# Around the second block's first norm, three units on each side run one half of the positions and then the other

## What is computed

```python
# end of the first block
f = (jax.nn.gelu(g, approximate=True) * a) @ w_down[l]      # (256, 2816) @ (2816, 1024)
x = x + rms_norm(f, norm_ffn_post[l])
# start of the second block
u = rmsnorm(x, norm_mix_g[l])
proj = u @ w_in[l]
(gq, gk, gv, gz, ga, gb, fq, fk, fv, ff, gate_a, gate_b) = jnp.split(proj, split_idx, axis=-1)
# both norms
y = xf * lax.rsqrt(jnp.mean(xf * xf, axis=-1, keepdims=True) + EPS)
return (y * g.astype(jnp.float32)).astype(x.dtype)
```

## Time and profile before

| | |
|---|---|
| median of 3 runs | 936.53 us (933.61 to 938.68) |
| the profiled execution, its own time | 933.1 us |
| its span, first to last instruction | 931.4 us |
| PE busy | 909.3 us, 98% of the span |
| DVE busy | 569.3 us, 61% |
| ACT busy | 498.1 us, 53% |
| POOL busy | 155.3 us, 17% |
| mean granted clock of TensorE | 0.998 |

### The profile page before, as it was taken

The page is one execution under the profiler, slowest core; times in us unless marked ns, Lnnn a source line. Parts: engine busy times, 40 slices in busy tenths (PEclk is TensorE's granted clock), DMA queues, the critical chain, the costliest instruction groups (busy, mean ns, idle before and its releaser), DMA issues.

```text
span 931.4 us, 15769 instructions
## 1 busy us (share of the span) xinstructions
PE 909.3 (98%) x6525; PEld 839.0 (90%) x6525; DVE 569.3 (61%) x817; ACT 498.1 (53%) x747; POOL 155.3 (17%) x169
## 2 busy tenths in 40 slices
PE   7999999999999999899999999999999999999998
PEld 7998999889999988787789997999999899998886
DVE  5556554778888753676446688765466665555442
ACT  5576864556665543557555673432545565564341
POOL 6011101511111100236634210000100001120000
PEclk9999999999999999999999999999999999999999
DMA  8743265565565556324534444632346547556560
GB/s 287 243 155 113 92 226 178 185 208 180 191 208 191 167 187 214 110 92 154 175 124 137 136 138 135 182 107 92 92 140 221 181 145 218 183 195 211 180 203 24
DMA packets 132123, 153.71 MB, mean 165 GB/s; under 512 B 9281, under 2 KB 105940, under 8 KB 132052
## 3 DMA queue, kind: packets, MB, share of 16 engines
q1 hardware_dynamic: 125684, 151.25, 50.3%
q10 hardware_dynamic: 6368, 1.45, 0.7%
HBM read 150.46 MB, written 2.23 MB: 164 GB/s over the span
## 4 chain that ended last, share of the span: by engine, by line
PE 85%; DVE 7%; ACT 3%; DMA 2%; issue 2%; POOL 1%; ACTq 0%; SPq 0%; POOLq 0%
PE ps L1830 75%; PE ps L1793 5%; PE ps L2046 2%; PE ps L1790 2%; DVE wl L798 2%; DVE gv L824 1%; ACT wh L1338 1%; DMA raw<-in_w_in 1%; DVE mt L1210 1%; DVE gv__83 L1040 0%; DMA U<-blocks 0%; PE ps L2022 0%; DVE xres L824 0%; DMA inverses<-Y 0%; ACT fg L1476 0%
## 5 line engine op out<-in xcount | busy, mean ns | idle before, releaser
L798 DVE TENSOR_TENSOR wl<-raw,wh 128x1024 fp32r<-128x1024 f32 (+1 forms) x272 | 323.8, 1206 | 202.6 <-ACT wh L1338 202.4
L1830 PE MATMUL ps<-xh,wh 128*128 128x256 f32 x1280 | 361.7, 283 | 1.4 <-ACT xh L1377 1.4
L1830 PE MATMUL ps<-xh,wl 128*128 128x256 f32 x1280 | 354.7, 277 | 1.2 <-DVE wl L798 1.2
L1830 PE MATMUL ps<-xl,wh 128*128 128x256 f32 x1280 | 351.5, 277 | 0.0
L1338 ACT ACTIVATE wh<-raw 128x1024 fp32r<-128x1024 f32 (+1 forms) x292 | 286.8, 1024 | 117.6 <-PE ps L1830 110.2
L1830 PEld LDWEIGHTS ps<-xh,wh 128*128 128x128 f32 x1280 | 241.3, 189 | 5.1 <-issue 2.4
L1830 PEld LDWEIGHTS ps<-xh,wl 128*128 128x128 f32 x1280 | 240.3, 188 | 1.6 <-DVE wl L798 1.6
L1830 PEld LDWEIGHTS ps<-xl,wh 128*128 128x128 f32 x1280 | 239.3, 188 | 0.3
L620 POOL TENSOR_TENSOR wl<-raw,wh 128x1024 fp32r<-128x1024 f32 (+1 forms) x20 | 53.0, 2649 | 76.6 <-ACT wh L1338 75.4
L1830 PE MATMUL ps<-wh,f2L 128*128 128x512 f32 x128 | 49.8, 389 | 0.0
L1830 PE MATMUL ps<-wh,f2H 128*128 128x512 f32 x128 | 49.8, 389 | 0.0
(11 more groups left out here) (316 smaller groups left out, 1371.3 us busy)
## 6 DMA issues: line engine op xcount, KB each, us to landing
raw<-in_w_in SPq DMA_DIRECT2D x56, 1024.0 KB, 5.0
raw<-in_w_up SPq DMA_DIRECT2D x38, 1024.0 KB, 5.2
raw<-in_w_down SPq DMA_DIRECT2D x26, 1024.0 KB, 5.0
raw<-in_w_out SPq DMA_DIRECT2D x8, 1024.0 KB, 5.0
raw<-in_w_proj_fox SPq DMA_DIRECT2D x4, 1024.0 KB, 5.3
raw<-in_w_proj_gdn SPq DMA_DIRECT2D x4, 1024.0 KB, 5.0
raw<-in_w_conv_branch SPq DMA_DIRECT2D x4, 512.0 KB, 3.4
raw<-in_w_att_branch SPq DMA_DIRECT2D x4, 512.0 KB, 3.3
```

The source lines that it names most:

```text
L798: e.tensor_tensor(L, R, H.bitcast(F32), ALU.subtract).then_inc(lo.sem)
L1830: k = e.matmul(o, l, r, start=opens, stop=done and n == ends[c], skip_group_check=True)
```

## The change

**PE's order.** Units 63, 64 and 65 (AHEAD2) now run for positions a = 0 first, all three, and then all three for a = 1. So do units 66, 67 and 68 (BEHIND2). A new function `part` issues the 12 matmuls of one unit and one half: all chunks high by high, the first two chunks with the low weights, all chunks with the low activations, the last two chunks with the low weights. The transposes of the norm (`x2_turn(a, h)`, four channel chunks of one half of positions) stand between these matmuls: (0, 0) before the last three of unit 65, (0, 1) in the middle of unit 66's first half, (1, 0) behind unit 68's first half, (1, 1) in the middle of unit 66's second half. The `warm` products of this norm are gone.

**The norm by halves.** The gain is now multiplied into XS by DVE (`x2_scaled`, with the row GN, loaded by one more DMA of 512 KB behind the first block's middle norm), and XH and XL are made in four pieces of 4 chunks by 128 positions (`x2_high`, `x2_low`), each from one PSUM bank.

**The other engines.** ACT, DVE and POOL have the order of this stretch written out. The second `low` halves of units 66 and 68 move to POOL; that of unit 67 stays with DVE, at another place. `small` begins behind unit 68 in place of unit 66. In the down projection the short unit (2 chunks) is now the first of a group, so units 59 and 65 have 4 chunks.

```diff
-POOL_HALF = frozenset([*range(26, 33), *range(74, 87)])
-LATE_LO = frozenset([33, 67])
+POOL_HALF = frozenset([*range(26, 33), 66, 68, *range(74, 87)])
+LATE_LO = frozenset([33])
...
-                unit_of(w_down[0], 4 * P * n, 4 if n < 5 else 2, 512 * i, "A",
-                        [pfg("fg", 4 + 2 * i + a) for a in range(2)] if n == 5 else None, k0=4 * n, first=n == 0)
+                k0 = max(4 * n - 2, 0)
+                unit_of(w_down[0], k0 * P, 4 if n else 2, 512 * i, "A",
+                        [pfg("fg", 4 + 2 * i + a) for a in range(2)] if n == 5 else None, k0=k0, first=n == 0)
...
+            e.dma_start(GN[:], norm_mix_g_2[0].partition_broadcast(P)).then_inc(ld_gn, 16)
...
@@ gpsimd
-            after_post(1)
+            for a in range(2):
+                rstd(prs, a, ss[:, 2 + a:3 + a], pred("sum", 2 + a))
+                e.wait_ge(*px("x", 2 + a))
+                rstd(nrs, a, ss[:, a:a + 1], nsq("sq", 4 + a))
+                low(U_FQ + 2 * a)
...
@@ vector
+            def x2_scaled(a):
+                e.wait_ge(*nrs("pow", 4 + a))
+                e.wait_ge(ld_gn, 16)
+                for k in (0, 512):
+                    e.scalar_tensor_tensor(XS[:, a, k:k + 512], XRES[:, a, k:k + 512], rs[:, 2 + a:3 + a], GN[:, k:k + 512],
+                                           ALU.mult, ALU.mult).then_inc(nsc.sem)
+
+            def x2_low(a, h):
+                e.wait_ge(*x2h("hi", 2 * a + h))
+                e.tensor_tensor(x2_part(XL, a, h), x2_ps(a, h), x2_part(XH, a, h).bitcast(F32), ALU.subtract).then_inc(x2l.sem)
...
+            post(1, U_FQ - 1, 1, 0)
+            low(U_FQ, 0)
+            x2_scaled(0)
+            low(U_FQ + 1, 0)
+            x2_low(0, 0)
+            post(1, U_FQ - 1, 1, 1)
+            x2_low(0, 1)
+            low(U_FQ + 1, 1)
+            low(U_FQ + 2, 0)
+            x2_scaled(1)
+            x2_low(1, 0)
+            x2_low(1, 1)
...
@@ scalar
+            post(1, U_FQ - 1, 1, 0)
+            e.wait_ge(*px("x", 2))
+            squares(0)
+            high(U_FQ, 0)
+            high(U_FQ, 1)
+            high(U_FQ + 1, 0)
+            x2_high(0, 0)
+            post(1, U_FQ - 1, 1, 1)
+            high(U_FQ + 1, 1)
+            x2_high(0, 1)
+            high(U_FQ + 2, 0)
+            e.wait_ge(*px("x", 3))
+            squares(1)
+            high(U_FQ + 2, 1)
+            keep_fqk(0)
+            x2_high(1, 0)
+            x2_high(1, 1)
...
@@ tensor
-            warm(WARM[0])
-            norm(2)
+            for a in range(2):
+                for u in AHEAD2:
+                    part(u, a, fH, fL, lambda a, q: fhi("hi", q // 2), lambda a, q: flo("lo", q // 2),
+                         at=3 if (u, a) == (U_FQ - 1, 1) else None, begins=lambda: x2_turn(0, 0))
+            part(U_FQ, 0, XH, XL, x2_hi, x2_lo, at=2, begins=lambda: x2_turn(0, 1))
+            part(U_FQ + 1, 0, XH, XL, x2_hi, x2_lo)
+            side.add(fox_norm(0))
+            part(U_FQ + 2, 0, XH, XL, x2_hi, x2_lo)
+            x2_turn(1, 0)
+            part(U_FQ, 1, XH, XL, x2_hi, x2_lo, at=2, begins=lambda: x2_turn(1, 1))
+            part(U_FQ + 1, 1, XH, XL, x2_hi, x2_lo)
+            side.add(fox_norm(1))
+            part(U_FQ + 2, 1, XH, XL, x2_hi, x2_lo)
             side.add(small())
```

214 lines of the change are left out of this document (155 added, 59 removed).

## The result

The changed kernel is slower: median 946.22 us (939.0 to 951.1, nine runs) against 937.2 (933.61 to 939.03, nine runs) of the kernel before on the same chip, ratio 1.0089 with a 95% interval of 1.0062 to 1.0116. The forecast was 932.0, with a range from 927.5 to 936.5. Two executions further on were in a slower state and are left out of their ratios: one of e4_cr_f4 (946.25 us) and one of e11_before_shift (1297.66 us, mean clock 0.654). All nine executions of the changed kernel had 0.982 to 0.992; those of the kernel before, in a later series of 30, had 0.992 to 1.000. So every execution of the changed kernel had a mean clock no higher than the lowest of that series.

What follows compares the result with a forecast made beforehand. PE, busy in 98% of the span, was taken to bound the kernel. Gross gain 8.8 us, minus 4.75 of new waits, plus 0.4 from later small work, gives 4.5: median 936.5 to 932.0, range 927.5 to 936.5.

Steps and rivals of the forecast that it cites:

- What is at stake, and the gross gain (8.8): Seam between the blocks: 10.8 us of PE time at stake, less 2.0 for transposes between products, leaves 8.8 us.
- The new waits at the seam: PE's waits in the new order, units 66 to 68: 0.2 + 0.95 + 0.25 + 2.4 + 0.95 = 4.75 us.
- The port: At the seam, DVE operations with two SBUF inputs and POOL's block each other; waits 4.75 us with it, 1.3 without.
- First transposes: no wait: At the seam, DVE's scalings end at 8.0, near the first transposes at 7.5; PE's wait was put at 0.
- rival 2: At the seam, POOL's first half takes the port before DVE's scaling; waits 6.2 us, time 934.5, chance 0.17.
- the waits for XH (0.2) and for XL (0.95 and 0.25): At the seam, PE waits 0.2 us for ACT's first XH piece, then 0.95 and 0.25 in unit 67.
- that for the low half of unit 68: In unit 68, PE waits 2.4 us for POOL's second low half, which starts only after DVE's scaling.
- The row at 406.64: Profile row before the change: POOL's 128x512 product took 2.71 us, not 1.30, inside two back-to-back DVE operations; basis for 4.75.
- The wait at fox norm 4: Three units later, the next half's norm stands on DVE behind a low half delayed by ACT's exponentials; PE waits 1.6 us.
- Rival 4: Units 74 and 75: POOL's low halves each come 3.1 us late; 2.1 us slower, 938.7, chance 0.04.
- The granted clock is full wherever PE works: Whole kernel: `warm` products only filled the gap, so removing them was costed at nothing.
- The cut of the down units: Down projection with the short unit first: same 132 products, ACT and DVE have idle time; costed at nothing.

Runs made afterwards that it cites:

- e4_cr_f4: e1_cr with DVE's scaling of fox norm 4 three ticks earlier, ahead of the low half that waits for ACT; 935.82 us, ratio 0.9996.
- e11_before_shift: The kernel before with Yt's start, levels and solves two ticks later; 934.47 us, ratio 0.9983.
- e10_shift: e9_all with Yt's start, levels and solves four ticks later on all engines; 928.54 us, ratio 0.9915 to the kernel before.
- e6_dve_lows: e1_cr with the second low halves of units 66 and 68 back on DVE; 934.76 us, ratio 0.996 to the kernel before.
- e8_down_split: The kernel before with only the new cut of the down projection, the short unit first; 935.52 us, ratio 0.9981.
- e2_warm: The changed kernel with 14 identity products on PE ahead of the wait for the second attention's bias; 936.84 us, ratio 1.0009 to the kernel before.
- e1_cr: The changed kernel with the second attention's bias three ticks earlier on POOL, ahead of unit 77's low half; 932.19 us, ratio 0.9969 to the kernel before.
- e7_e3_late: e4_cr_f4 with the exponentials' last product four ticks later on POOL, behind the root of fox norm 5; 934.8 us, ratio 0.9975 to the kernel before.
- e3_before_late: The kernel before with five extra 64x256 products on POOL ahead of the second attention's bias; 945.12 us, ratio 1.011.
- e5_before_cr: The kernel before with e1_cr's edit, the second attention's bias earlier on POOL; 933.72 us, ratio 0.9983.
- e9_all: e6_dve_lows with the two edits of e4_cr_f4 and e7_e3_late; 931.96 us, ratio 0.9956 to the kernel before.
- e12_fill: e1_cr with nine identity products ahead of the seam's first transposes and fourteen ahead of fox norm 4's; 931.87 us, ratio 0.9961 to the kernel before.

## Why the prediction was wrong, step by step

The forecast's size at the seam was right; the lead was lost at three places behind it (fox norm 4, the attention's bias, Yt). The third goes with a small transfer that took 4.2 us in this execution, and is not shown to be the change's.

**What held.**
- *What is at stake, and the gross gain (8.8).* e10_shift has PE 9.8 us ahead of before at fox norm 4's transposes (248.57 - 238.76). Of these 2.0 are the later waits of 1.3 and 0.7 that are gone, and 0.8 of the seam's new waits are still in it: 9.8 - 2.0 + 0.8 = 8.6. It keeps 7.2 at the bias of the attention (266.50 - 259.26) and 8.4 at the end (741.87 - 733.47).
- *The new waits at the seam* were put at 4.75 and measured at 1.89 + 1.33 + 0.78 = 4.0. With the later small work still open the forecast had PE 8.8 - 4.75 + 2.0 = 6.05 us ahead just before fox norm 4's wait. It was 6.6.
- *The port* between DVE and POOL is the reason for most of these waits: with POOL's two low halves back on DVE, 0.8 of the 4.0 us are left (e6_dve_lows).

**Right in sum, wrong in place.** "First transposes: no wait" failed. It was rival 2's mechanism: POOL's half began 0.15 us ahead of DVE's scaling, which the prediction argued against because DVE's next operation would be ready at that moment. It was ready, and POOL had begun. The price was 1.9 us and not 2.3. In turn the waits for XH (0.2) and for XL (0.95 and 0.25) did not come, that for the low half of unit 68 was 1.33, not 2.4, and the last one for XH 0.78, not 0.95. That the sum came out 0.75 off is in part luck. The row at 406.64, from which the choice was made, showed POOL arriving inside a DVE operation and being held by the next one as well. Here POOL arrived inside DVE's operations too (372.47, 383.87), and both times it went ahead of the next one. One row was not enough to choose by.

**The wait at fox norm 4** was put at 1.6 and was 2.74. The mechanism is the one forecast: DVE stands for 3.77 us at a low half whose high half follows the exponentials on ACT, and the norm's scaling is behind it. Timeline of DVE after:

```profile
430.70 1.23 DVE L843 TENSOR_TENSOR wl<-raw,wh 128x1024 fp32r<-128x1024 f32 x1 [3.77 <-ACT wh L1420]
...
433.97 0.68 DVE L1059 TENSOR_TENSOR fkm<-fkm,gv__83 128x512 f32<-128x512 f32 x1
```

The clock behind it (1.6 us more) was not in the sum.

**The step that failed: the sum ended there.** Having moved PE 6 us ahead of POOL, DVE and ACT, the prediction followed it for six units and not to the next thing that these engines owe it. Its 8.8 - 4.75 + 0.4 has no term behind fox norm 4, which is the same as a term of 0, and the runs show 3.1 us of waiting and 5.7 us of clock there. What these engines owed was the attention's bias, three units further on, and the profile before had its margin in plain sight: a wait of 0.46 us at 455.64, which is no margin at all. Rival 4 had the engine and the units right ("POOL falls behind in units 74 and 75"), but looked for the harm in the low halves, where PE did not wait, and not in the operation queued behind them. It gave it 0.04. Its time, 938.7, was also too small, because:

**"The granted clock is full wherever PE works" was false,** and this was the costliest sentence. From 6.6 us ahead to 9.1 behind is 15.7 us; 1.6 + 5.7 of them are lost to the clock behind two waits, and some 1.5 behind a third. The trace before had contradicted it: behind its own 3.25 us wait the granted clock is 0.57 from 380 to 384 us, and eight transposes take 1.40 us, where they take 1.09 at full clock (e8_down_split, and e11_before_shift behind the same wait). The prediction looked only at stretches without waits. The `warm` products that "only filled the gap" were not idle decoration. The change took them out at the seam, and e2_warm shows what filling one gap, another one, is worth: 7.5 us by the ratios, and 4.2 in the two profiles at the transposes of the first probabilities.

**The cut of the down units** "at nothing" was 1.5 us of the gap by e8_down_split and e11_before_shift (2.1 against the profiled execution of before, which also lost some to the clock). It does not change the sum, which went by the whole gap, but a part of what was credited to the two halves can be had by this alone.

GN's transfer was at nothing and showed no wait in any profile.

## What to carry to other kernels

When a change moves the engine that bounds the kernel ahead of its helpers, list what each helper owes it next, with the margin that the profile shows, until a place where the lead is used up; a wait of 0.5 us in the profile before is a margin of zero, and the whole lead turns into idle time there. Price an idle stretch of the matrix engine by the clock behind it too, not only by its length: here 3.5 us of idle time cost 3.1 us by themselves and 5.7 by the clock behind them. And order the helpers' operations by who is waited for: one such move (e1_cr) was worth some 11 us by the ratios and 9.5 between the two profiles, and the last version, which is the change with a handful of them, is 0.85% faster than before.

## What the runs showed of the hardware

- **The clock falls behind short waits, and not each time.** Behind the waits of 0.5 us at the attention it was 1.00 in every profile. Behind the same 1.9 us at the seam it fell in the profiled executions of e1_cr and e7_e3_late (0.79 and 0.77) and not in those of the changed kernel, e2_warm and e4_cr_f4 (1.00). With what was lost behind the seam's next waits, 8 us on (e1_cr 0.58, e7_e3_late 0.59 and e2_warm 0.83 from 390 to 394), the seam took 2.7, 2.5 and 1.5 us longer in these three than in the other two. Behind 2.7 us it fell in all four that have this wait. Behind the 3.25 us at the seam of the kernels without the change it fell in three profiles (before, e3_before_late, e5_before_cr, for about 3 us) and not in the fourth (e11_before_shift). Behind 3.5 us (changed kernel) it stood at 0.50 for some 12.5 us (456.94 to 469.4), though PE had work, and behind 4.8 us (e3_before_late) for about 13. Why it took so much longer there was not tried.
- **Two operations of DVE back to back, and one of POOL's that comes inside the first.** POOL was held by both at 406.64 (2.71 us in place of 1.30) and at 381.80 (1.29 in place of 0.19), and went ahead of the second at 372.47 and 383.87 (a scaling of 0.74 us took 2.86). In the first two DVE's next operation was a low half, in the other two a scaling; whether that is the reason was not tried.
- **A scatter that the granted clock does not show.** In the stage of the up projection (220 to 300 us) a product of 256 columns takes 276 ns in most profiled executions and 281 in others, with the next starting 4% later, at a granted clock of 1.00 in both. PE's group in e10_shift, then in e9_all:

```profile
L1948 PE MATMUL ps<-xh,wh 128*128 128x256 f32 x236 | 65.2, 276 | 0.0
```

```profile
L1948 PE MATMUL ps<-xh,wh 128*128 128x256 f32 x227 | 63.8, 281 | 0.0
```

  It is 4.5 us by the time PE reaches the seam, in e8_down_split, e9_all and e12_fill, kernels whose code is the same up to there, or nearly so. The kernel before has runs around 934 and around 938 at the same mean clock, which may be this. Its cause stays open. For a comparison of two profiles it means: put both on a zero right ahead of the change.
